# Four small gaps in on-chip memory behind the split weight tiles of a float32r kernel

## The reference

```python
# first block: modulation by a conditioning vector, then
z = modulate(rmsnorm(x, norm1_g), shift1, scale1) @ w_in + b_in      # 1024 -> 2048
y = [spatial gating over chunks of 128 | causal conv of width 31]    # two halves of 512
x = x + gate1 * (y @ w_out)
g, up = split(modulate(rmsnorm(x, norm2_g), shift2, scale2) @ w_ffn_in)   # 1024 -> 2 x 2816
x = x + gate2 * ((silu(g) * up) @ w_ffn_out)                         # 2816 -> 1024
x = modulate(rmsnorm(x, norm_f_g), shift_f, scale_f)
# second block, two layers: attention (8 forgetting heads, 8 sparse heads) or a pooling mixer, then
h = h + rmsnorm(swiglu(rmsnorm(h, g2), w_gate, w_up, w_down), g3)
```

## Time and profile before

| | |
|---|---|
| two executions | 1759.5 and 1761.01 us, median 1760.26 us |
| span of the profiled execution (first to last instruction) | 1757.1 us; no other time of it is given |
| TensorE, matmuls | 1679.6 us busy (96%), 8263 records |
| TensorE, weight loads | 1311.8 us (75%), 8263 records, beside the matmuls |
| VectorE | 916.1 us (52%) |
| ScalarE | 627.2 us (36%) |
| GpSimd | 225.3 us (13%) |
| DMA | 179.27 MB, mean 102 GB/s |

### The profile page before, as it was taken

One profiled execution on the slowest core, in us unless ns is written; L12 is line 12 of the kernel. 1 busy time (PEld: TensorE's weight loads), 2 busy tenths in 40 slices (PEclk: granted clock), 3 DMA queues, 4 the chain that ended last, 5 costly groups with the idle time before them and its releaser, 6 DMA issues.

```text
span 1757.1 us, 22185 instructions
## 1 busy us (share of the span) xinstructions
PE 1679.6 (96%) x8263; PEld 1311.8 (75%) x8263; DVE 916.1 (52%) x1376; ACT 627.2 (36%) x946; POOL 225.3 (13%) x204
## 2 busy tenths in 40 slices
PE   1999899999999999999999999999998999999996
PEld 1757688888888867666667788888887688888885
DVE  6765676544334463666667544444336644444223
ACT  1324334222223362554555333333226333333221
POOL 5010106998000030000000000003000000000000
PEclk9999999999999999999998999999999899999998
DMA  7565134454332241111101322233211133333221
GB/s 281 204 200 167 40 110 161 169 181 157 109 107 97 69 117 64 37 37 49 37 25 61 108 96 95 95 100 115 98 57 49 61 98 100 99 96 115 92 80 48
DMA packets 48588, 179.27 MB, mean 102 GB/s; under 512 B 5968, under 2 KB 6640, under 8 KB 48272
## 3 DMA queue, kind: packets, MB, share of 16 engines
q1 hardware_dynamic: 43600, 162.04, 27.5%
q0 software_dynamic: 3776, 14.78, 2.7%
q10 hardware_dynamic: 1152, 1.66, 0.4%
HBM read 173.04 MB, written 2.10 MB: 100 GB/s over the span
## 4 chain that ended last, share of the span: by engine, by line
PE 71%; issue 22%; DVE 5%; DMA 1%; ACT 1%; ACTq 1%; POOL 0%; POOLq 0%; DVEq 0%; SPq 0%
PE bank L383 15%; PE bank L385 14%; PE bank L384 14%; PE bank L1437 3%; PE bank L1439 2%; PE bank L1438 2%; PE bank L1545 2%; PE bank L1501 2%; PE bank L1521 2%; DVE ada_acc L1972 1%; PE bank L1172 1%; PE bank L1174 1%; PE bank L1173 1%; PE bank L454 1%; PE bank L1394 1%
## 5 line engine op out<-in xcount | busy, mean ns | idle before, releaser
L309 DVE TENSOR_TENSOR w_lo<-raw,w_hi 128x1024 fp32r<-128x1024 f32 (+1 forms) x229 | 316.4, 1382 | 575.2 <-ACT w_hi L305 574.9
L305 ACT ACTIVATE w_hi<-raw 128x1024 fp32r<-128x1024 f32 (+1 forms) x229 | 258.0, 1127 | 564.4 <-PE bank L385 482.7
L383 PE MATMUL bank<-h_hi,w_hi 128*128 128x512 f32 x1136 | 448.0, 394 | 0.5 <-DVE w_lo L309 0.5
L385 PE MATMUL bank<-h_hi,w_lo 128*128 128x512 f32 x1136 | 442.2, 389 | 0.0
L384 PE MATMUL bank<-h_lo,w_hi 128*128 128x512 f32 x1136 | 442.2, 389 | 0.0
L383 PEld LDWEIGHTS bank<-h_hi,w_hi 128*128 128x128 f32 x1136 | 213.2, 188 | 50.2 <-issue 5.2
L385 PEld LDWEIGHTS bank<-h_hi,w_lo 128*128 128x128 f32 x1136 | 213.2, 188 | 45.0
L384 PEld LDWEIGHTS bank<-h_lo,w_hi 128*128 128x128 f32 x1136 | 213.3, 188 | 44.6 <-issue 1.7
L383 PE MATMUL bank<-hid_hi,w_hi 128*128 128x512 f32 x528 | 205.6, 389 | 0.0
L384 PE MATMUL bank<-hid_lo,w_hi 128*128 128x512 f32 x528 | 205.4, 389 | 0.0
L385 PE MATMUL bank<-hid_hi,w_lo 128*128 128x512 f32 x528 | 205.4, 389 | 0.0
(11 more groups left out here) (397 smaller groups left out, 2079.5 us busy)
## 6 DMA issues: line engine op xcount, KB each, us to landing
raw<-in_f2i SPq DMA_DIRECT2D x88, 512.0 KB, 3.3
raw<-in_ffi SPq DMA_DIRECT2D x44, 512.0 KB, 3.4
raw<-in_f2o SPq DMA_DIRECT2D x32, 704.0 KB, 4.0
ada_w<-in_ada_w SPq DMA_DIRECT2D x24, 512.0 KB, 4.3
m_out<-in_ada_w POOLq DMA_DIRECT2D x24, 512.0 KB, 3.7
raw<-in_att_w SPq DMA_DIRECT2D x23, 512.0 KB, 3.3
raw<-in_ffo SPq DMA_DIRECT2D x16, 704.0 KB, 4.0
raw<-in_ada_w SPq DMA_DIRECT2D x16, 512.0 KB, 4.9
```

The lines of the kernel that those rows point to most:

```text
L305: nc.scalar.activation(WH[par][:, 0:kc * P], RAW[s][:, 0:kc * P], ACT.Copy).then_inc(whi, count)
L309: nc.vector.tensor_tensor(WL[par][:, 0:kc * P], RAW[s][:, 0:kc * P], WH[par][:, 0:kc * P].bitcast(F32), ALU.subtract).then_inc(wlo, count)
L383: pe_.matmul(bank[:, :], w_h, hi[:, k0 + k, :], start=start and k == 0, stop=False)
L385: last = pe_.matmul(bank[:, :], w_l, hi[:, k0 + k, :], start=False, stop=stop and k == kc - 1)
```

## The change

Four tiles that nothing reads or writes are placed behind the four split weight tiles. No instruction, order, wait, size or data type of the kernel is changed; only addresses are.

```diff
-        WH = [sb(f"w_hi{i}", [P, KH * P], F32R) for i in range(2)]
-        WL = [sb(f"w_lo{i}", [P, KH * P], F32R) for i in range(2)]
+        W4 = []
+        for name, gap in (("w_hi0", 24), ("w_hi1", 16), ("w_lo0", 24), ("w_lo1", 8)):
+            W4.append(sb(name, [P, KH * P], F32R))
+            sb("behind_" + name, [P, gap])
+        WH, WL = W4[:2], W4[2:]
         X = sb("x_res", [P, C, S])
```

## The result

The changed kernel takes 1787.7 us in the median (1787.53 to 1787.88), the kernel before 1760.26; the ratio is 1.0154, 95% interval 1.0135 to 1.0173. It is slower by 27 us. I had forecast 1760 us in a range of 1744 to 1776, so the forecast and the range both failed.

A forecast was written before the change was run, and what follows sets the result against it. The prediction took the pace of TensorE's matmul stream (226.6 ns a float32r matmul) to bound the kernel. All terms were put at 0 us, so it forecast the median, 1760 us, with a range of 1744 to 1776 us.

The forecast's parts named there:

- The count of 5808: All matmuls of the six large float32r groups and their fellows; at 226.6 ns they are 1316 us, 75% of the span.
- the one from float32 to float32r: Float32r matmuls with unequal remainders: taken as 0 us, as float32 convolution equals the aligned row; bounds were -62 and +41 us.
- The sign that I had named for it: Matmul stream: a pace that moved while float32 lines 454 and 1601 kept theirs would prove the float32-to-float32r step wrong.
- the bound of 1 ns a record: Float32r matmuls: the rows bound a price of alignment at 1 ns a record, 6 us, giving the range 1754 to 1766.
- two readings that I called undecided: Float32r matmuls: whether alignment or the data type pays for the 10.6 ns above the 216 ns of float32.
- the crowded read: Not a name in the prediction; nearest there: each weight load of 512 bytes is read while 2048 column bytes are read.
- pooling and convolution change their remainders too: Other matmuls of raw weights: unequal against equal remainders priced at 2 ns in 430 a group, taken as 0 us.
- The first reading for the data type: Float32r stream: the excess ignores where slices lie above 512 bytes; all buffers and slices run at one pace to 0.1 ns.
- The reads do collide: Rival, float32r matmuls: weight and column reads collide, new remainders part them; 226.6 to 216 ns, 1698 us; chance 0.13.
- The rival that ended slower: Every float32r matmul: column slices beginning off a boundary cost one more piece, 7.1 ns each, 1801 us; chance 0.07.
- a harm to one weight tile of four: Rival: only one weight tile's remainder matters, a quarter of 5808 at 10.6 ns, 15 us; 1745 or 1776 us; chance 0.04.
- splits beside the stream: ScalarE and VectorE splits at new remainders: 0 us, any ns covered by some 2.5 us of slack per split.

The follow-up runs named there:

- sweep2: Kernel of bare matmuls, none of the reference, over data types, sizes and offsets; per matmul float32 429 ns, bfloat16 216, float32r 227 at equal offsets, 232.5 at 4 bytes.
- all_shift: Against the kernel before: one gap of 288 bytes ahead of the split weight tiles, so weight and column tiles move together; 1760.8 us, ratio 1.0001.

## Why the prediction was wrong

**What bounds the kernel** was right: the pace of the matmul stream alone moved the time. The count of 5808 was too large by the attention stage's 384, which lost 0.7 ns each and not 5.5.

**The step that failed** is the one from float32 to float32r: "I take 0, since the row nearest in kind with unequal remainders (the convolution) equals the aligned one". That term of the sum, put at 0, measured 5.5 ns a matmul and 27 us. The sign that I had named for it came: the pace moved while float32 lines kept theirs. The float32 rows were read rightly, since float32 is at 429 ns for every offset in `sweep2` too. But they say nothing of float32r, which pays 2 to 8 ns a matmul where its two operands stand apart by 32, 64 or 96 bytes. From the same rows came the bound of 1 ns a record and with it my own range of 1754 to 1766. Of the two readings that I called undecided, the crowded read has this for it: float32r and bfloat16 both go over their columns once, and the one with four bytes an element pays for distance while the one with two doesn't; and at the lower clock float32r doesn't pay either (0.42 to 0.43 us at unequal remainders). The Trainium skill's "TensorE: Matmul & The Clock Gate", section "Step-by-step: what each phase is for", has the two read ports of TensorE independent, so that a load takes nothing from a running matmul. The float32 and bfloat16 lines agree with that. The float32r lines don't (227 ns at equal offsets, 233 at a distance of 64 bytes), and the measurement decides.

A smaller error stands beside it: I wrote that pooling and convolution change their remainders too. They do by themselves, but not against each other, so they could have shown nothing either way.

**The first reading for the data type** was a trap. That every slice and both buffers run at one pace to 0.1 ns showed no insensitivity: all those slices had the same distance by 256 bytes, so the trace held one point of the curve, and it was the lowest.

**The rivals.** "The reads do collide" was half right: they meet, but the new remainders made it worse. I had tied that mechanism to a gain, because I took equal remainders for the collision; they are the case with the lowest pace. The rival that ended slower had the right sign and the wrong mechanism (a boundary of the columns themselves; `all_shift` excludes it). Its 7.1 ns were near the 5.5 measured by chance. I gave slower 7 in 100 and left it out of the range, which stopped at 1776 because I priced a harm to one weight tile of four, while all four came to stand apart from the columns.

**The rest**: dead tiles 0 us, float32 products within 1 ns, splits beside the stream, blocks of DMA landing in 4.1 us (`ada_w`) and 3.7 (`m_out`), all as forecast.

## What to carry to other kernels

In a dense stream of float32r matmuls of 512 columns keep the weight slices and the column slices at the same remainder by 256 bytes, and check it whenever a tile of odd size is put between them: here 64 bytes cost 0.9% and 288 bytes 1.9%. When all rows of a trace stand at one value of the thing that a change varies, they bound nothing, however many and however regular they are; a bare loop over that value costs 200 us of chip time.

## What the runs showed of the hardware that I had not expected

Float32r with 128x128 weights and 512 columns has a locked rhythm of 226.7 ns at 2.4 GHz and falls out of it to between 228 and 239 ns; which of the two it is in can depend on the matmuls before (227 or 233 ns at the same 16 bytes). The excess over 213.3 ns (512 columns at 2.4 GHz) stays about as large with fewer columns. Line 99 of `sweep2` has 256 columns at equal offsets:

```profile
108.30 2.07 PE L99 MATMUL bank<-c,w 128*128 128x256 f32 x16
110.20 2.05 PE L100 MATMUL bank<-c,w 128*128 128x256 f32 x16
```

1.90/16 = 119 ns is 12 ns above 106.7; for 512 columns it is 13.4. But the price of distance is gone here: line 100 has 256 columns with the weights 64 bytes past them, and with line 101 starting at 112.09 it costs 1.89/16 = 118. With 384 columns 64 bytes cost 2 ns (lines 97 and 98). Float32 and bfloat16 have 2 to 3 ns above theirs. Which part of the read path makes the rhythm, and why 4 bytes suffice to break it, stays open: these runs show the price and its period, not the banks behind it.
